# A recurrent block with its gates in two halves, branch tiles between them, and one buffer slot for each branch tile

## What is computed

```python
u = x @ w_in
gate_br, rec_br = u[..., :D_RNN], u[..., D_RNN:]
rec, conv_state = causal_dwconv(rec_br, conv_w, conv_b, conv_prev)      # width 4
r = sigmoid(blockdiag(rec, ga_w) + ga_b);  i = sigmoid(blockdiag(rec, gx_w) + gx_b)   # 4 blocks of 256
log_a = -8 * r * softplus(-lam)
a = exp(log_a);  u = sqrt(-expm1(2 * log_a)) * i * rec
h_t = a_t * h_{t-1} + u_t                                               # scan over time
out = (h * gelu(gate_br)) @ w_out
```

## Time and profile before

| | value |
|---|---|
| median of three runs | 1748.54 us (1742.39 to 1749.49) |
| the profiled execution: its own time, its span | 1739.84 us, 1738.2 us |
| PE busy | 1616.9 us, 93% |
| DVE busy | 997.8 us, 57% |
| ACT busy | 716.7 us, 41% |
| POOL busy | 304.1 us, 17% |
| granted TensorE clock, mean over the span | 0.964 |

### The profile page before, as it was taken

One profiled execution on the slowest core, in us unless ns is written; L12 is line 12 of the kernel. 1 busy time (PEld: TensorE's weight loads), 2 busy tenths in 40 slices (PEclk: granted clock), 3 DMA queues, 4 the chain that ended last, 5 costly groups with the idle time before them and its releaser, 6 DMA issues. The chain is left out here.

```text
span 1738.2 us, 31445 instructions
## 1 busy us (share of the span) xinstructions
PE 1616.9 (93%) x12602; PEld 1573.3 (91%) x12602; DVE 997.8 (57%) x1552; ACT 716.7 (41%) x1310; POOL 304.1 (17%) x758
## 2 busy tenths in 40 slices
PE   8999798978979999999998998799899999999985
PEld 8999677858979999999998998799899999999985
DVE  3345667754885445536557594758753464455662
ACT  4345666843444234323334337334342332243341
POOL 4610333530032012102200000002220120021000
PEclk9999899988999999999999999899899999999988
DMA  7644000052212222222221221231222222223211
GB/s 261 130 138 157 1 1 1 1 189 81 74 61 87 96 77 93 86 86 85 96 86 61 85 86 61 67 115 52 85 86 85 86 86 87 84 89 105 73 61 64
DMA packets 39946, 148.01 MB, mean 85 GB/s; under 512 B 6304, under 2 KB 6320, under 8 KB 39360
## 3 DMA queue, kind: packets, MB, share of 16 engines
q1 hardware_dynamic: 33264, 121.26, 21.6%
q0 software_dynamic: 6544, 24.81, 4.1%
HBM read 140.57 MB, written 9.10 MB: 86 GB/s over the span
## 5 line engine op out<-in xcount | busy, mean ns | idle before, releaser
L1821 PE MATMUL PS<-XH,HI 128*128 128x272 f32 (+1 forms) x1936 | 411.4, 294 | 42.7 <-DVE XL L1101 14.1
L1821 PE MATMUL PS<-XH,LO 128*128 128x272 f32 (+1 forms) x1936 | 405.0, 291 | 0.0
L1821 PE MATMUL PS<-XL,HI 128*128 128x272 f32 (+1 forms) x1936 | 404.0, 290 | 0.0
L1821 PEld LDWEIGHTS PS<-XH,HI 128*128 128x128 f32 x1936 | 310.6, 191 | 46.9 <-DVE LO L449 26.1
L443 ACT ACTIVATE HI<-RAW 128x1024 fp32r<-128x1024 f32 x223 | 235.4, 1057 | 279.0 <-PE PS L1821 256.0
L1821 PE MATMUL PS<-GH,HI 128*128 128x272 f32 (+1 forms) x1504 | 319.5, 294 | 25.3 <-DVE LO L449 9.6
L449 DVE TENSOR_TENSOR LO<-RAW,HI 128x1024 fp32r<-128x1024 f32 x223 | 272.1, 1221 | 100.8 <-ACT HI L443 100.5
L1821 PE MATMUL PS<-GH,LO 128*128 128x272 f32 (+1 forms) x1504 | 314.1, 291 | 0.0
L1821 PE MATMUL PS<-GL,HI 128*128 128x272 f32 (+1 forms) x1504 | 313.9, 290 | 0.0
L1821 PEld LDWEIGHTS PS<-XL,HI 128*128 128x128 f32 x1936 | 308.8, 191 | 0.1
L1821 PEld LDWEIGHTS PS<-XH,LO 128*128 128x128 f32 x1936 | 307.4, 190 | 0.0
(11 more groups left out here) (362 smaller groups left out, 1941.4 us busy)
## 6 DMA issues: line engine op xcount, KB each, us to landing
RAW<-in_w_stream SPq DMA_DIRECT2D x223, 512.0 KB, 3.3
ARENA<-in_cache_cmp POOLq DMA_DIRECT2D x32, 128.0 KB, 3.1
out_win_old<-in_win_copy POOLq DMA_DIRECT2D x1, 4064.0 KB, 18.5
X<-in_x SPq DMA_DIRECT2D x4, 544.0 KB, 7.0
X<-in_x POOLq DMA_DIRECT2D x1, 2176.0 KB, 9.1
out_y<-X POOLq DMA_DIRECT2D x1, 2176.0 KB, 6.9
ARENA<-in_cache_sel POOLq DMA_DIRECT2D x16, 128.0 KB, 2.8
ARENA<-in_cache_win POOLq DMA_DIRECT2D x4, 512.0 KB, 5.1
```

The lines of the kernel that those rows point to most:

```text
L1821: ins = mm(PS[0:rows, b + h, 0:width], w[:, 0:rows], cols(x, x0 + n, h), start=first, stop=last)
```

## The change

- PE's order becomes: gate tiles of n = 0 to 3, branch tiles 0 and 1, gate tiles of n = 4 to 7, branch tiles 2 to 7. The gate weights are laid out so that each chunk holds a and x of two n.
- ACT's exponentials and roots are done for four n at a time. The branch tiles 0, 1 and 2 are first copied out of PSUM as they are and get their gelu later, in place; the others get it from PSUM.
- The branch values have a slot each (`GB`, eight slots, at the address of `GL`) instead of two slots in `RTM`.
- DVE scans the first four n while the gates of the other four are under way; the sample steps are done in two halves.
- Softplus goes to the end of layer 0, in three steps between the updates of its last eight tiles, with ACT's small exponential after the fourth of them.

```diff
-            section("rgate", 16, lambda n: "act", lambda n: [2 * (n // 8) + n % 2])
-            section("gbr", 8, lambda n: "act", one)
+            section("rgate0", 8, lambda n: "act", lambda n: [n // 4])
+            section("gbr0", 2, lambda n: "act", one)
+            section("rgate1", 8, lambda n: "act", lambda n: [n // 4])
+            section("gbr1", 6, lambda n: "act", one)
...
+        GB = nc.alloc_sbuf_tensor_at("GB", [P, KT * TOK], F32, offset=GL_AT)[:, :]
...
 ACT, in tail(), gate tile k of layer 0:
                         s.activation(XH3[:, k, :], X3[:, k, :], ACT.Copy).then_inc(in_hi, 1)
+                        if k == 3:
+                            act.wait_ge(lam_ready, 1)
+                            s.activation(SMALL[:, 40:48], SMALL[:, 40:48], ACT.Exp, scale=-1.0).then_inc(sp_ready, 1)
...
 ACT, the block:
-            for n in range(8):
-                s.activation(RR3[:, n, :], RR3[:, n, :], ACT.Exp, scale=SMALL[:, 48 + n:49 + n]).then_inc(a_ready, 1)
-            for n in range(8):
-                s.activation(VV3[:, n, :], VV3[:, n, :], ACT.Sqrt).then_inc(sqrt_ready, 1)
...
+            def branch_copy(n):
+                o = branch_tile(n)
                 act.wait_ge(tile_done, o + 1)
-                if n >= 2:
-                    act.wait_ge(prod_done, GATED0 + n - 1)
-                else:
-                    act.wait_ge(m_ready, 8)
-                s.activation(halves(RTM[:, (n % 2) * TOK:(n % 2 + 1) * TOK]), banks(o), ACT.Gelu_apprx_tanh)\
-                    .then_inc(act_took, 1)
+                s.activation(halves(GB3[:, n, :]), banks(o), ACT.Copy).then_inc(act_took, 1)
                 splits.after(o)
+            def branch_gelu(n):
+                ...
+                s.activation(GB3[:, n, :], GB3[:, n, :], ACT.Gelu_apprx_tanh).then_inc(gb_copied, 1)
...
+            for n in range(4):
+                gate_values(n)
+            decay(0, 4)
+            branch_copy(0)
+            input_root(0, 4)
+            branch_copy(1)
+            for n in range(4, 8):
+                gate_values(n)
+            decay(4, 8)
+            branch_copy(2)
+            input_root(4, 8)
+            for n in range(3):
+                branch_gelu(n)
+            branch(3)
+            branch(4)
+            for n in range(3):
+                gated_hi(n)
+            branch(5)
+            gated_hi(3)
+            gated_hi(4)
+            branch(6)
+            gated_hi(5)
+            branch(7)
+            gated_hi(6)
+            gated_hi(7)
...
 DVE, in tail():
+                        if k == 2:
+                            lambda_size()
+                        elif 4 <= k < 7:
+                            softplus(k - 4)
...
 DVE, the block:
+            for n in range(4):
+                gate_input(n)
+            for n in range(4):
+                decayed_input(n)
+            scan(0)
+            scan(1)
+            splits.after(branch_tile(0))
+            scan(2)
+            scan(3)
+            gate_input(4)
+            splits.after(branch_tile(1))
+            gate_input(5)
+            chain.did(sample_steps(0))
+            gate_input(6)
+            gate_input(7)
+            for n in range(4, 8):
+                decayed_input(n)
+            for n in range(4, 8):
+                scan(n)
+                if n == 5:
+                    splits.after(branch_tile(2))
+            sample_steps(1).then_inc(h_ready, 1)
+            dve.wait_ge(h_ready, 9)
+            splits.after(branch_tile(3))
+            for n in range(8):
+                gated(n)
+                if n > 3:
+                    splits.after(branch_tile(n))
+                if n:
+                    gated_lo(n - 1)
+            gated_lo(7)
```

More of the change, by code:

```diff
@@ L300, in build, with gate_tile, branch_tile @@
         EXT0 = (4, 4 + 48 + 4)
+        def gate_tile(n):
+            return O0["rgate0"] + 2 * n if n < 4 else O0["rgate1"] + 2 * (n - 4)
+        def branch_tile(n):
+            return O0["gbr0"] + n if n < 2 else O0["gbr1"] + n - 2
         def group(n):
@@ new lines, in input_root @@
+            def input_root(lo, hi):
+                for n in range(lo, hi):
+                    s.activation(VV3[:, n, :], VV3[:, n, :], ACT.Sqrt).then_inc(sqrt_ready, 1)
+            def branch_copy(n):
+                o = branch_tile(n)
+                act.wait_ge(tile_done, o + 1)
+                s.activation(halves(GB3[:, n, :]), banks(o), ACT.Copy).then_inc(act_took, 1)
+                splits.after(o)
+            def branch_gelu(n):
+                o = branch_tile(n)
+                act.wait_ge(act_took, taken(o)[1])
+                s.activation(GB3[:, n, :], GB3[:, n, :], ACT.Gelu_apprx_tanh).then_inc(gb_copied, 1)
@@ L1086, in _, with branch, gated_hi @@
+            def branch(n):
+                o = branch_tile(n)
+                act.wait_ge(tile_done, o + 1)
+                s.activation(halves(GB3[:, n, :]), banks(o), ACT.Gelu_apprx_tanh).then_inc(act_took, 1)
+                splits.after(o)
+            def gated_hi(n):
                 act.wait_ge(prod_done, GATED0 + n + 1)
                 s.activation(GH3[:, n, :], REC3[:, n, :], ACT.Copy).then_inc(mid_hi, 1)
+            for n in range(4):
+                gate_values(n)
+            decay(0, 4)
@@ L1681, in _ @@
             v.memset(SMALL[:, 7:8], 0.0).then_inc(lam_ready, 1)
[L1682 to L1705, removed]
             rg0 = MID_COUNT["rec"]
@@ L1740, in _, with gate_input @@
             dve.wait_ge(mid_lo, rg0 + 8)
-            for n in range(8):
-                o = O0["rgate"] + 2 * n
+            def gate_input(n):
+                o = gate_tile(n)
+                splits.after(o)
                 dve.wait_ge(act_took, taken(o + 1)[1])
@@ L1772, in _ @@
[L1772 to L1782, removed]
-                    .then_inc(prod_done, 1)
-                splits.after(o)
+            l3 = LAST.rearrange("p (k c) -> p k c", k=8)
@@ L1785, in _, with gated, gated_lo @@
+            def gated(n):
+                if n < 3:
+                    dve.wait_ge(gb_copied, n + 1)
+                else:
+                    dve.wait_ge(act_took, taken(branch_tile(n))[1])
+                v.tensor_tensor(REC3[:, n, :], REC3[:, n, :], GB3[:, n, :], ALU.mult).then_inc(prod_done, 1)
+            def gated_lo(n):
                 dve.wait_ge(mid_hi, MID_COUNT["gated"] + n + 1)
@@ L2171, in _, with gates @@
                      each=(lambda k: pe.wait_ge(in_lo, IN_COUNT["x1"] + k + 1)) if n == 0 else None)
-            for n in range(8):
+            def gates(n):
                 pe.wait_ge(mid_lo, MID_COUNT["rec"] + 2 * (n // 2) + 2)
+                c = C0["rgate0"] + n // 2 if n < 4 else C0["rgate1"] + n // 2 - 2
                 for gate in range(2):
-                    tile(O0["rgate"] + 2 * n + gate, C0["rgate"] + 2 * (n // 4) + gate, (2 * (n % 4), 2 * (n % 4) + 1),
-                         GH3, GL3, 2 * (n // 2))
-            for n in range(8):
-                tile(O0["gbr"] + n, C0["gbr"] + n, range(KT), XH3, XL3, 0)
+                    w = 4 * (n % 2) + 2 * gate
+                    tile(gate_tile(n) + gate, c, (w, w + 1), GH3, GL3, 2 * (n // 2))
+            for n in range(4):
+                gates(n)
+            for n in range(2):
+                tile(branch_tile(n), C0["gbr0"] + n, range(KT), XH3, XL3, 0)
+            for n in range(4, 8):
+                gates(n)
+            for n in range(2, 8):
+                tile(branch_tile(n), C0["gbr1"] + n - 2, range(KT), XH3, XL3, 0)
             for n in range(8):
```

100 lines of the change are left out of this document (71 added, 29 removed).

## The result

The changed kernel took 1728.43 us, the median of four runs (1727.9 to 1730.5), against 1746.15 for the kernel before (1742.39 to 1749.49, four runs). The ratio is 0.9902, 95% interval 0.988 to 0.9924: faster by about 1%. In a second series (six runs) it was 0.988 (0.9855 to 0.9904). The profiled execution took 1728.4 us, its span 1726.8.

The account below looks back on a forecast made before the run. PE bounds the kernel, busy 93%, losing time to PSUM tiles not taken out. The block's 72.3 + 4.7 = 77.0 us against 98.6 gains 21.6; 1748.5 - 21.6 = 1726.9, forecast 1726, range 1716 to 1737.

Parts of the forecast that it names:

- rival A: Gates: the clock drops after PE's 2.8 us first wait, price 2.3 us; gain 19.3, time 1729; chance 0.23.
- 2.8 + 0.2 + 0.75 + 0.9: PE's remaining waits in us: first sigmoid, ACT's order in first gates, start of second gates, sigmoid of n = 6.
- a load of 5.06 us: Second half: 5.06 us from low part freeing a buffer to next high part, so PE waits 0.9.
- 72.3: Block: us PE needs at full rate for 16 gate tiles of 1.51 and 8 branch tiles of 6.03.
- Operations worth 0: Moving softplus from the block's start to layer 0's tail: 0 to 0.1 us, as DVE's convolutions catch up.
- The table load: Before the first gate's sigmoid: the 1.28 us load goes, PE's wait shrinks from 4.17 to about 2.8 us.
- B, the end is late: Branch 6, 7 and start of rg_out: PE stands 3 to 6 us; gain 17, time 1732; chance 0.13.
- C, the switch of tables: ACT loses another 1.28 us at each table load; gain 14.5, time 1734; chance 0.04.
- D, the clock stays low: Short gate waits keep 1.2 GHz through both halves and three branch tiles: +34 us, time 1761; chance 0.03.
- E, the slots free nothing: ACT in its order still waits for scans, PE stands 11 us; gain about 10, time 1738; chance 0.07.
- No wait is for a matmul operand: Block before the change: PE stands only because a PSUM tile has not been taken out; 19.7 us idle.
- the range's low end (1716): Whole time: lower bound, taken from the profiled time with the larger gain.

Follow-up runs that it names:

- slots and the new order: Kernel before with eight branch slots, ACT taking four branch tiles before the first GH, DVE's low parts between scans; ratio 0.9948, 1733.37 us.
- the first profile: The kernel before, unchanged, in the profile the prediction was read from; profiled execution 1739.84 us.

## Why the prediction was right, and where it was off

- *Size and sign.* Forecast 1726, measured 1728.4 and 1726.8 in two series, gain 21.6 forecast and 20.2 in the block. The range 1716 to 1737 held it. The mechanism that came is rival A's, which had 0.23: the gain lies between its 19.3 and the forecast's 21.6.
- *The waits.* Forecast 2.8 + 0.2 + 0.75 + 0.9 = 4.7; measured 2.70 and 0.78, and in place of the 0.2 and the 0.9 two delays of 0.3 (1061.16, 1086.56) that the profile doesn't list as waits. Both come from the same order on ACT: sigmoid, a high part, tanh, and only then the sigmoid that frees the next tile's banks. The mechanism of each was right but the last: it rested on a load of 5.06 us that would hold ACT's high part behind the gates of n = 5. That high part (1084.13) waited for nothing, 4.5 us after DVE freed the buffer at 1079.66 (1078.46 + 1.20). 5.06 was read at a place where ACT waited for a load, and I took it for a constant.
- *The term that was mis-sized is the clock.* I took no drop after the first wait and put it in rival A with 0.23. It did drop, in all four profiles with a wait of 2.7 us, and cost 1.6 us (A said 2.3, after 4.17). So the number lies between: 72.3 + 3.5 + 1.6 and 1.0 at starts of gate tiles, 78.4 instead of 77.0. Of the 72.3 itself, 16 × 1.51 + 8 × 6.03 is 72.4. Two rows at 3.35 us, one at either rate, gave no ground for 0.50 against 0.23.
- *Softplus.* Operations worth 0, as forecast, but only just. In the changed kernel the last convolution waits for PE's last `rec` tile and starts 0.92 us after the first gate matmul. In the kernel before DVE never stands between its eight convolutions, and the last starts 0.98 us after it (1039.59 and 1038.61): DVE has caught up to within 0.1 us at the last tile. The table load was priced at 1.28 and was 1.5, and 2.5 to 2.7 with the low level behind it.
- *B, the end is late.* It wasn't. The margins of branch 6 and 7 came out at 1.0 and 0.6 (forecast 1.2 and 0.8), the last `GL`'s at 1.2 (0.8). They are as thin as said: 4.3 us on DVE cost 5.1.
- *C, the switch of tables.* Refuted: 1068.05 after 1066.76, 1073.49 after 1072.19, 1079.37 after 1078.07. By the Trainium skill, "ScalarE: Activation LUTs", section "What ACT_TABLE_LOAD costs", a drain of some 1380 ns would stand at each; no row here has it.
- *D, the clock stays low.* Refuted: 0.98 over the stretch.
- *E, the slots free nothing.* Its mechanism is real and the kernel avoids it: with the old order ACT waits for the scans one instruction later and the gain is 0.
- *A sentence that was wrong without a price.* "No wait is for a matmul operand" does not hold: the 1.5 us for L449 is a wait for a low part of weights. The 19.7 us include it; it still stands with slots and the new order and is gone in the changed kernel.
- *What I carried over right by luck.* The kernel before stood at a median of 1748.54 in three runs and at 1746.15 with the fourth, 2.4 us less than the forecast started from. I added the gain to the median because the profiled execution was 8.7 us below it. The reason, an execution with the clock up for longer in attention, I did not look for, and the range's low end (1716) rested on it.

## What to carry to other kernels

When PE waits for PSUM, read the order of the engine that empties it before adding buffers: here eight slots were worth nothing, a new order with them 10 us, and one copy moved behind three others 4.4 us. Price a wait of PE of 2.7 us or more with the low level behind it, mostly 1.6 to 2.4 us here. Before comparing two whole times, cut both spans at the same instructions: a gain of 20 us can stand beside 8 us that come from elsewhere.

## What was not expected of the hardware

- The granted clock fell to 0.84 with PE busy 10.00 of 10 us, and did so in two of the three profiles of that window shown above. By its records PE is busy without a pause in all three from 130 to 170 us. Just ahead of the fall stand 32 narrow matmuls of 32 columns (153.87 to 157.36 in the kernel before, profiled again; those of 288 columns take 0.44 us instead of 0.30 from 158.34 on), and the same 32 stand in the first profile (155.59 to 159.08) with no fall behind them. What decides stays open.
- A wait of 3.35 us left the rate at full in the earlier trace rows; at the same place in the kernel before, profiled again, and in the changed kernel the first pair took 0.82 after 3.36 and 3.34 us. A wait's length alone doesn't decide.
- After 3.27 us of waiting PE made four pairs at the full rate before the low level set in (1118.59), after 2.70 us it began at once (1053.72).
